# Gate rows first in a layer, and the output-gate products in halves between the steps of the matrix-memory core

## The chip, the cores and the metric

The kernel runs on one core of a Trainium2 chip. It is one program that goes twice through a loop over layers. The metric is the device time of one execution in microseconds (us); the time before is the median of three runs. Engines are called as in the profile: PE is TensorE (with PEld its weight loads), DVE is VectorE, ACT is ScalarE, POOL is GpSimd, SP is SyncE, which here only issues DMAs.

## What is computed

One inference step of a two-layer decoder. Each layer mixes 512 prompt tokens and 32 sampled tokens (8 sequences of 4), so N = 544 columns, by two mixers side by side, and then applies a feed-forward block. The part at issue is the matrix-memory mixer (mLSTM), with 4 heads of width 128:

```python
h = rmsnorm(x, W['norm1_g'][l])
u, v, o, ig, fg, q, kv, ng, ga, gb = split_cols(h @ W['w_in'][l])
...
c, conv_new = causal_conv(u, conv_buf, conv_w, conv_b)
q = jnp.einsum('bthd,hde->bthe', c, w_mq)
k = jnp.einsum('bthd,hde->bthe', c, w_mk) * (M_HEAD_DIM ** -0.5)
pre = jnp.concatenate([ig, fg], axis=-1).astype(jnp.float32) + b_gates.astype(jnp.float32)
i_pre = pre[..., :M_HEADS]
log_f = jax.nn.log_sigmoid(pre[..., M_HEADS:])
h, C, n, m = mlstm_chunkwise(q, k, v, i_pre, log_f, C0, n0, m0)
h = h * lax.rsqrt(jnp.mean(h * h, axis=-1, keepdims=True) + EPS) * norm_g...
out = h.reshape(B, T, M_WIDTH) * jax.nn.sigmoid(o.astype(jnp.float32))
```

`ig` and `fg` are the gate rows (8 rows in all): from them come, per token, the decays that the core needs. `o` is the output gate (512 rows): its sigmoid is needed only at the very end of the mixer, when the normalized core output is multiplied by it.

## The kernel before, in words

Every engine has its own instruction list, written out by hand; waits are on semaphores, and nothing but these lists and waits sets the order. Activations are kept feature-major: `hT` is the normed input as 8 chunks of 128 features by 544 columns. Weights arrive as units of 128 x 1024 floats (512 KB) in the order of the table `UNITS`, through a ring of 8 slots in SBUF that SP fills in order; before a slot is filled again SP waits in `unit_used` for its last user. A product writes a pair of PSUM banks (two halves of 272 columns); the table `GROUPS` numbers the products, and number modulo 4 is the pair. `begin` makes PE wait until that pair was read.

Some products are plain f32. The output gate, and many later ones, run in three passes of a split format: ACT casts a weight unit to a high part (`split_high`), DVE subtracts to get the low part (`split_low`), and likewise the input becomes `xh` (by ACT) and `xl` (by DVE; it takes the place of `hT`, so it must come after the last read of `hT`). `passes` then issues high times high, high times low and low times high, for each chunk and half: 48 matmuls of 272 columns per product.

A layer's first part is, on PE: the norm sum (L778); the four products `u` (L768, the first paced chunk by chunk by DVE, which writes `hT`); the value rows `tm` in token-major form (L826, L827); the gate rows `if` (L836); the four output-gate products `o` (L806); the query and key products `mq` and `mk` (L852), which ACT copies out (L1249); transposes of the gate rows (L863, wait for ACT's exponentials `wexp_ready`); the weighted keys `kw` (L872), which DVE copies out (L1543). Then comes the matrix-memory core: 4 heads of 5 steps, k = 0 to 19, with j = k modulo 5. In step k PE does the score product of step k+1 (L896), at j = 2 two spreads of gate rows over the partitions for the next head (L885, 4 rows of weights), then numerator and denominator of step k (L910, L911; at j = 4 eight 4-column products with the old state, L918), and at j = 4 the new state (L930, 32 rows). ACT makes the exponentials, DVE masks and multiplies them with the scores (`st_ready`) and, after a head's end, takes the reciprocal of its denominator (L1578). After the core PE sums the prompt state (L956), ACT copies it out (L1288), splits two query units (L1192), squares the heads' outputs (L1297), and PE takes their means (L968, `mn`); then the query products follow (L806).

ACT's chain for the gate rows (L1227 to L1233) and DVE's scans (L1511 to L1528) lie before the core and end in `rows_ready`.

## Time and profile before

| what | us |
|---|---|
| median of 3 runs | 2261.07 (2256.67, 2261.07, 2265.15) |
| the profiled execution: span from the first to the last instruction | 2255.4 |
| PE busy (share of the span) | 2113.5 (94%) |
| DVE, ACT, POOL busy | 934.4, 678.8, 103.4 |
| mean granted TensorE clock | 0.931 of 2.4 GHz |

The profile gives one execution; its span is what it has of that execution's own time, and the three timed runs lie 1.3 to 9.8 us above it. A busy PE is not PE at its peak: the ends of matmuls are modelled, and the granted clock is either 1.0 (2.4 GHz) or 0.5 (1.2 GHz), so that a stretch's mean says how much of it ran at which.

### The profile page before, as it was taken

The page shows a single profiled execution, that of the slowest core. Times are in us where ns is not written, and L with a number is a line of the kernel's source. Part 1 is how long each engine was busy: PE and PEld are TensorE (multiplying, and loading weights), DVE is VectorE, ACT ScalarE, POOL GpSimd, SP SyncE. Part 2 cuts the span into 40 slices and gives each one's busy share as a digit, 9 for nine tenths or more (in the row PEclk, how much of TensorE's full clock was granted, in tenths as well). Part 3 has the DMA queues.
Part 4 walks back from the last instruction along what each step waited for, and adds up shares of the span by engine and source line. Part 5 has one row for each costly group of instructions (what it writes and reads, how often), then busy time and mean ns, then how long its engine had stood idle before and what let it go on. Part 6 is the DMA issues. An engine that isn't in the chain of part 4 may idle for free. (4 is left out here: it accounts for less than half of the span.)

```text
span 2255.4 us, 34271 instructions
## 1 busy us (share of the span) xinstructions
PE 2113.5 (94%) x14028; PEld 1829.3 (81%) x14028; DVE 934.4 (41%) x1592; ACT 678.8 (30%) x1287; POOL 103.4 (5%) x144
## 2 busy tenths in 40 slices
PE   6989999999997999999779899999999979999996
PEld 5575884569997999999755758745799979999995
DVE  3144655643335332333222356556333453323333
ACT  2342235642223221222114323356422232212221
POOL 0012111000000000000000121110000000000000
PEclk9997897979998999999989979979799989999998
DMA  6211143002221222221042012510122212222211
GB/s 249 75 48 38 62 151 104 1 20 86 92 85 63 88 85 94 85 87 64 15 169 103 19 47 87 155 65 1 37 86 85 94 57 89 90 85 93 86 48 40
DMA packets 48114, 176.31 MB, mean 78 GB/s; under 512 B 6506, under 2 KB 6538, under 8 KB 47506
## 3 DMA queue, kind: packets, MB, share of 16 engines
q1 hardware_dynamic: 40754, 144.80, 19.0%
q0 software_dynamic: 7200, 29.27, 3.8%
q8 instruction: 114, 1.87, 0.3%
q14 instruction: 46, 0.38, 0.1%
HBM read 163.46 MB, written 14.71 MB: 79 GB/s over the span
## 5 line engine op out<-in xcount | busy, mean ns | idle before, releaser
L806 PE MATMUL ps<-xh,late_w 128*128 128x272 f32 x3840 | 650.0, 290 | 17.6 <-DVE xl L1803 15.7
L806 PEld LDWEIGHTS ps<-xh,late_w 128*128 128x128 f32 x3840 | 547.9, 190 | 21.3 <-issue 17.3
L1466 DVE TENSOR_TENSOR late_w<-ring,late_w 128x1024 fp32r<-128x1024 f32 x196 | 240.3, 1226 | 735.9 <-ACT late_w L1192 735.9
L1192 ACT CAST late_w<-ring 128x1024 fp32r<-128x1024 f32 x196 | 205.3, 1048 | 831.0 <-PE ps L806 830.9
L806 PE MATMUL ps<-xl,late_w 128*128 128x272 f32 x1920 | 398.8, 289 | 0.0
L806 PEld LDWEIGHTS ps<-xl,late_w 128*128 128x128 f32 x1920 | 304.8, 190 | 0.0
L806 PE MATMUL ps<-ah,late_w 128*128 128x272 f32 x1408 | 234.7, 288 | 0.0
L806 PEld LDWEIGHTS ps<-ah,late_w 128*128 128x128 f32 x1408 | 198.7, 188 | 0.0
L1331 ACT ACTIVATE slab<-ps,stat 128x31 f32<-128x31 f32 (+5 forms) x204 | 84.3, 449 | 117.2 <-DVE stat L1698 117.2
L806 PE MATMUL ps<-mh,late_w 128*128 128x272 f32 x576 | 98.9, 288 | 0.0
L996 PE MATMUL ps<-slab 64*128 64x512 f32 (+2 forms) x192 | 94.1, 618 | 0.0
L1033 PE MATMUL ps<-slab,vkv 128*64 128x256 f32 x320 | 91.3, 430 | 0.0
L1033 PEld LDWEIGHTS ps<-slab,vkv 128*64 128x64 f32 x320 | 44.2, 151 | 51.2 <-issue 34.9
L806 PEld LDWEIGHTS ps<-mh,late_w 128*128 128x128 f32 x576 | 82.4, 189 | 0.1
L768 PE MATMUL ps<-slab,ring 128*128 128x272 f32 x256 | 62.4, 407 | 21.2 <-DVE slab L1478 19.8
L826 PE MATMUL ps<-ring,slab 128*128 128x512 f32 (+1 forms) x160 | 81.7, 592 | 0.0
L806 PE MATMUL ps<-al_first,late_w 128*128 128x272 f32 x384 | 79.3, 288 | 0.0
L768 PEld LDWEIGHTS ps<-slab,ring 128*128 128x128 f32 x256 | 50.4, 198 | 33.9 <-issue 21.3
L1341 ACT ACTIVATE slab<-slab,stat 128x128 f32<-128x128 f32 (+4 forms) x140 | 69.0, 555 | 10.7 <-DVE stat L1721 10.4
L1015 PEld LDWEIGHTS ps<-const,slab 128*128 128x128 f32 (+1 forms) x384 | 42.9, 143 | 34.8 <-issue 23.4
L1015 PE MATMUL ps<-const,slab 128*128 128x128 f32 (+1 forms) x384 | 60.2, 297 | 6.6 <-ACT slab L1341 6.6
L806 PE MATMUL ps<-al_rest,late_w 128*128 128x272 f32 x320 | 66.2, 288 | 0.0
(298 smaller groups left out, 2911.8 us busy)
## 6 DMA issues: line engine op xcount, KB each, us to landing
ring<-in_W SPq DMA_DIRECT2D x262, 512.0 KB, 3.3
slab<-in_pages POOLq DMA_DIRECT2D x64, 128.0 KB, 2.5
slab<-in_c POOLq DMA_DIRECT2D x8, 512.0 KB, 9.5
out_sC<-slab POOLq DMA_DIRECT2D x8, 512.0 KB, 2.9
slab<-in_win POOLq DMA_DIRECT2D x2, 2048.0 KB, 8.6
out_oldwin<-in_cwin POOLq DMA_DIRECT2D x2, 2016.0 KB, 14.1
xT<-in_xT SPq DMA_DIRECT2D x8, 272.0 KB, 4.5
out_y<-slab SPq DMA_DIRECT2D x8, 272.0 KB, 2.1
```

The lines of the kernel that those rows point to most:

```text
L768: mm = pe.matmul(out[:, a, :], w[:, k, :], src[:, k, a * NHALF:(a + 1) * NHALF], start=(k == 0), stop=(k == kcs - 1))
L806: mm = pe.matmul(out[:, a, :], w[:, k * P:(k + 1) * P], x[:, a * NHALF:(a + 1) * NHALF], start=start, stop=stop)
L826: pe.matmul(ps[0:rows, s, :], x, w[:, 0:512], start=(k == 0), stop=(k == KC - 1))
L996: mm = pe.matmul(out[:, r], qrT[hd, r0 + r, i * P:(i + 1) * P], kT[hd, brs[0] - 1:brs[-1], 0:(i + 1) * P], start=True, stop=True)
L1015: mm = pe.transpose(ps[0:rows, 5 + x % 2, at:at + P], part, ident)
L1033: mm = pe.matmul(out, vkv[:, j, (br - 1) * P + g * HD:(br - 1) * P + (g + 1) * HD], PT[:, x % 2, 2 * c * P:2 * (c + 1) * P], start=(br == ...
L1192: act.copy(hi, ring[:, u % RING, :]).then_inc(wh_ready, 1)
L1331: ins = act.activation(prob(k)[:, r, :], score(k)[:, r, :], ACT.Exp, bias=stat[:, k % 3, r:r + 1], accum_out=stat[:, 3 + k % 3, r:r + 1] i ...
L1341: ins = act.activation(prob(k)[:, r, :], prob(k)[:, r, :], ACT.Copy, scale=stat[:, 8 + k % 3, r:r + 1])
L1466: dve.tensor_tensor(lo, ring[:, u % RING, :], hi.bitcast(F32), ALU.subtract).then_inc(wl_ready, 1)
```

## The change

In a layer, `if` comes first on PE, and is now the product that DVE's writes of `hT` pace; ACT's chain for the gate rows follows at once, before it reads out `u`. The four `o` products no longer stand between `if` and `mq`. Each is cut into two halves of 272 columns (`fill`: 24 matmuls into bank 5), and the eight halves stand on PE ahead of the numerator of the steps k = 0, 2, ..., 14. ACT copies each half out after its exponential of the next step, without the sigmoid, and takes one sigmoid over all four after the core. The split weights of `o` move into ring slots 1 to 4 (the last four `tm` units), so units after `o` get other slots, and SP holds the first `k` unit until all fills are done. The small product with `blk` moves behind the next head's first numerator (`new_n`), since bank 5 is now the fills'.

```diff
-UNITS = ([("u", m) for m in range(4)] + [("tm", k) for k in range(KC)] + [("if", 0)]
+UNITS = ([("if", 0)] + [("u", m) for m in range(4)] + [("tm", k) for k in range(KC)]
...
+FILL_BANK = 5
+FILLS = [(m, a) for m in range(4) for a in range(2)]
+def fill_at(k):
+    return k // 2 if k % 2 == 0 and k // 2 < len(FILLS) else None
...
+                        if UNITS[n] == ("k", K_ORDER[0]):
+                            sp.wait_ge(fill_done, len(FILLS))
...
+                    w = landed(("if", 0)).rearrange("p (k m) -> p k m", k=KC)
+                    out = begin(("if", 0))
+                    for k in range(KC):
+                        pe.wait_ge(h_ready, k + 1)
...
                     for m in range(4):
-                        fm("u", m, ready=(h_ready, 0))
+                        fm("u", m)
...
-                    for m in range(4):
-                        product3(("o", m), ("o", m), xh, xl, (xl_ready, 0)).then_inc(pair_done, 1)
+                    def fill(x):
+                        m, a = FILLS[x]
+                        n = SPLIT[("o", m)]
+                        pe.wait_ge(wl_ready, n + 1)
+                        if x >= 1:
+                            pe.wait_ge(fill_free, x)
+                        wh, wl, _ = split_weights(n)
+                        half = slice(a * NHALF, (a + 1) * NHALF)
+                        for k in range(KC):
+                            if x == 0:
+                                pe.wait_ge(xl_ready, k + 1)
+                            for w, y, start, stop in ((wh, xh, k == 0, False), (wh, xl, False, False), (wl, xh, False, k == KC - 1)):
+                                mm = pe.matmul(ps[:, FILL_BANK, 0:NHALF], w[:, k * P:(k + 1) * P], y[:, k, half], start=start, stop=stop)
+                        mm.then_inc(fill_done, 1)
...
+                        if fill_at(k) is not None:
+                            fill(fill_at(k))
                         numden(k)
+                        if j == 0 and h >= 1:
+                            new_n(h - 1)
...
-                    for m in range(4):
-                        if m < 2:
-                            split_high(m + 2)
-                        out, free = done(("o", m))
-                        act.activation(halves(haT[:, m, :]), out, ACT.Sigmoid).then_inc(free, 1)
...
+                        if k >= 1 and fill_at(k - 1) is not None:
+                            m, a = FILLS[fill_at(k - 1)]
+                            act.wait_ge(fill_done, fill_at(k - 1) + 1)
+                            act.copy(haT[:, m, a * NHALF:(a + 1) * NHALF], ps[:, FILL_BANK, 0:NHALF]).then_inc(fill_free, 1)
+                            if a == 1 and m < 2:
+                                split_high(m + 2)
...
+                    act.wait_ge(fill_free, len(FILLS))
+                    act.activation(haT[:, :, :], haT[:, :, :], ACT.Sigmoid).then_inc(sig_ready, 1)
...
-                    split_low(2)
-                    split_low(3)
+                    split_low(0)
+                    split_low(1)
+                    dve.wait_ge(pair_done, GROUP[("tm", TT)] + 1)
+                    for k in range(KC):
+                        dve.wait_ge(xh_ready, k + 1)
+                        dve.tensor_tensor(xl[:, k, :], hT[:, k, :], xh[:, k, :].bitcast(F32), ALU.subtract).then_inc(xl_ready, 1)
```

On PE, at the start of a layer, before (L768 is `u`, L826 and L827 are `tm`):

```order
L778 MATMUL ps<-acc,ones 128x272 x2
L768 MATMUL ps<-slab,ring 128x272 x64
L826 MATMUL ps<-ring,slab 128x512
L827 MATMUL ps<-ring,slab 128x280
L826 MATMUL ps<-ring,slab 128x512
```

and of the change (L862 is `if`, L810 is `u`, L876 and L877 are `tm`):

```order
L820 MATMUL ps<-acc,ones 128x272 x2
L862 MATMUL ps<-slab,ring 64x272 x16
L810 MATMUL ps<-slab,ring 128x272 x64
L876 MATMUL ps<-ring,slab 128x512
L877 MATMUL ps<-ring,slab 128x280
```

The 16 matmuls of `if` now stand ahead of the 64 of `u`. On PE, in the first head's steps 2 to 4, before (L910 and L911 are numerator and denominator, L899 and L896 scores, L918 the 4-column products):

```order
L910 MATMUL ps<-slab 128x256
L911 MATMUL ps<-slab,ones 128x256
L899 MATMUL ps<-slab 32x32
L910 MATMUL ps<-slab 128x128
L911 MATMUL ps<-slab,ones 128x128
L896 MATMUL ps<-slab 128x512
L914 MATMUL ps<-slab 128x32
L918 MATMUL ps<-slab 128x4 x8
```

and of the change (L898 are the fills, of which the last row of one and the first three of the next are shown):

```order
L898 MATMUL ps<-xh,gwl 128x272
L966 MATMUL ps<-slab 128x256
L967 MATMUL ps<-slab,ones 128x256
L955 MATMUL ps<-slab 32x32
L966 MATMUL ps<-slab 128x128
L967 MATMUL ps<-slab,ones 128x128
L952 MATMUL ps<-slab 128x512
L898 MATMUL ps<-xh,gwh 128x272
L898 MATMUL ps<-xl,gwh 128x272
L898 MATMUL ps<-xh,gwl 128x272
```

The order of the core's own rows is the same; 24 rows of a fill stand ahead of step 2 and of step 4. On ACT, after the core, before (L1267 and L1288 are copies out of PSUM, L1192 splits query units, L1297 squares):

```order
L1267 COPY slab<-ps 128x512
L1288 COPY slab<-ps 128x512
L1192 CAST qwh<-ring 128x1024 x2
L1297 ACTIVATE sq<-slab 128x544 x4
L1302 ACT_TABLE_LOAD
```

and of the change:

```order
L1331 COPY slab<-ps 128x512
L1358 COPY slab<-ps 128x512
L1360 ACT_TABLE_LOAD
L1360 ACTIVATE slab<-slab 128x2176
L1261 CAST qwh<-ring 128x1024 x2
L1369 ACTIVATE sq<-slab 128x544 x4
L1374 ACT_TABLE_LOAD
```

A table load and one sigmoid over 2176 columns now stand ahead of the splits and the squares.

## Rows read from the trace of the kernel before

**Rows 1.** The page's head: the span, and each engine's busy time.

```profile
span 2255.4 us, 34271 instructions
```

**Rows 2.** PE's waits, summed: waiting line, what it waited for, total, times, longest.

```profile
PE ps L885 <- ACT slab L1259: 6.0, 8, 0.8
```

**Rows 3.** PE by time, start of the first layer: start, length, row, idle before.

```profile
19.75 8.96 PE L768 MATMUL ps<-slab,ring 128*128 128x272 f32 x32 [5.37 <-DVE slab L1478]
30.14 22.27 PE L768 MATMUL ps<-slab,ring 128*128 128x272 f32 x96 [1.43 <-DMA ring<-in_W]
```

**Rows 4.** PE by time, from the gate rows to the core, first layer.

```profile
105.66 7.55 PE L836 MATMUL ps<-slab,ring 128*64 128x272 f32 x32
114.11 0.48 PE L806 MATMUL ps<-xh,gwh 128*128 128x272 f32 x2 [0.91 <-DVE xl L1506]
...
128.56 0.82 PE L806 MATMUL ps<-xh,gwh 128*128 128x272 f32 x2 [2.21 <-DVE gwl L1466]
...
130.08 0.66 PE L806 MATMUL ps<-xh,gwh 128*128 128x272 f32 x2
130.53 0.66 PE L806 MATMUL ps<-xl,gwh 128*128 128x272 f32 x2
...
142.11 3.83 PE L852 MATMUL ps<-slab,small 128*128 128x272 f32 x16
146.31 3.93 PE L852 MATMUL ps<-slab,small 128*128 128x272 f32 x16 [0.37 <-ACT slab L1249]
...
157.39 1.18 PE L885 MATMUL ps<-acc,const 4*128 4x272 f32 x4 [1.75 <-DVE slab L1543]
```

**Rows 5.** PE by time, the same place in the second layer.

```profile
1226.78 7.55 PE L836 MATMUL ps<-slab,ring 128*64 128x272 f32 x32
...
1261.74 3.83 PE L852 MATMUL ps<-slab,small 128*128 128x272 f32 x16
```

**Rows 6.** Windows: both cores of the program's two layers, and 4 us of the first.

```profile
157.40:246.20 88.80, 85.78 (x296) 54.61 (x296) 45.12 (x88) 18.85 (x48) 21.53 (x17) 0.73 0.10 36
177.00:179.00 2.00, 2.00 (x19) 1.98 (x18) 0.00 (x0) 0.00 (x0) 0.00 (x0) 1.00 0.00 0
181.00:183.00 2.00, 2.00 (x4) 0.67 (x3) 1.97 (x8) 0.20 (x1) 0.64 (x1) 0.50 0.00 0
1277.00:1366.00 89.00, 85.79 (x296) 54.64 (x296) 45.31 (x89) 19.03 (x49) 21.56 (x17) 0.73 0.10 36
```

The columns are: from and to, length, busy time of PE, PEld, DVE, ACT and POOL with their instructions, granted clock, share of the DMA engines, GB/s.

**Rows 7.** PE by time, in the core of the first layer and behind it.

```profile
176.93 1.95 PE L918 MATMUL ps<-slab 128*128 128x4 f32 x16
...
179.48 3.71 PE L930 MATMUL ps<-slab 32*128 32x512 f32 x4
...
249.41 6.51 PE L968 MATMUL ps<-sq,ones 128*128 128x272 f32 x16 [3.21 <-ACT sq L1297]
```

**Rows 8.** ACT by time, first layer.

```profile
106.58 1.99 ACT L1192 CAST gwh<-ring 128x1024 fp32r<-128x1024 f32 x2
...
122.75 0.62 ACT L1239 ACTIVATE slab<-ps 128x544 f32<-128x544 f32 x1
...
142.95 1.28 ACT L1242 ACT_TABLE_LOAD   x1
...
145.66 2.61 ACT L1249 ACTIVATE slab<-ps 128x544 f32<-128x544 f32 x5
...
246.72 1.99 ACT L1192 CAST qwh<-ring 128x1024 fp32r<-128x1024 f32 x2
248.61 1.20 ACT L1297 ACTIVATE sq<-slab 128x544 f32<-128x544 f32 x2
```

**Rows 9.** DVE by time, first layer.

```profile
113.24 5.17 DVE L1506 TENSOR_TENSOR xl<-slab,xh 128x544 fp32r<-128x544 f32 x8 [3.23 <-PE ps L836]
...
127.29 2.34 DVE L1466 TENSOR_TENSOR gwl<-ring,gwh 128x1024 fp32r<-128x1024 f32 x2
...
182.63 3.54 DVE L1578 RECIPROCAL slab<-slab 128x544 f32<-128x544 f32 x1
```

More of the change, by code:

```diff
@@ L80, with slot, turn, earlier @@
 UCOLS = 1024
+TURNS = UNIT[("q", 0)]
+def slot(n):
+    return n % RING if n < TURNS else (n - TURNS + UNIT[("o", 0)]) % RING
+def turn(n):
+    return sum(slot(x) == slot(n) for x in range(n))
+def earlier(n):
+    return max((x for x in range(n) if slot(x) == slot(n)), default=None)
 TMC = 512 + 280
-GROUPS = ([("n1", 0)] + [("u", m) for m in range(4)] + [("tm", i) for i in range(TT + 1)] + [("if", 0)]
-          + [("o", m) for m in range(4)] + [(w, h) for h in range(MH) for w in ("mq", "mk")]
+GROUPS = ([("n1", 0), ("if", 0)] + [("u", m) for m in range(4)] + [("tm", i) for i in range(TT + 1)]
+          + [(w, h) for h in range(MH) for w in ("mq", "mk")]
           + [("aw", 0)] + [("kw", i) for i in range(TT + 1)]
@@ L209, in al @@
             return al_first[:, k, :] if k < AL_FIRST else al_rest[:, k - AL_FIRST, :]
+        ring_at = where()
         ring = sb("ring", [P, RING, UCOLS])
+        gate_w = tuple(nc.alloc_sbuf_tensor_at(name, [P, 2, UCOLS], F32R, offset=ring_at + 4 * at * UCOLS)
+                       for name, at in (("gwh", 1), ("gwl", 3)))
         const = sb("const", [P, CONST_W])
@@ L321, in bc @@
             return ap.to_broadcast(shape)
+        assert [slot(UNIT[("tm", k)]) for k in range(4, KC)] == [1, 2, 3, 4] == [slot(UNIT[("k", m)]) for m in K_ORDER]
+        assert not {slot(UNIT[(w, m)]) for w in ("o", "q") for m in range(4)} & {1, 2, 3, 4}
         cos, sin, ident = con("cos"), con("sin"), con("ident")
@@ L371, in build_step @@
         h_ready = sem("h_ready")
+        fill_done = sem("fill_done")
+        fill_free = sem("fill_free")
+        sig_ready = sem("sig_ready")
+        n0_done = sem("n0_done")
         conv_ready = sem("conv_ready")
@@ L744, in landed @@
                         n = UNIT[key]
-                        pe.wait_ge(unit_landed[n % RING], 16 * (n // RING + 1))
-                        return ring[:, n % RING, :]
+                        pe.wait_ge(unit_landed[slot(n)], 16 * (turn(n) + 1))
+                        return ring[:, slot(n), :]
                     def begin(key):
@@ L812, in fm @@
                         product((kind, m), (kind, m), src, kcs, ready=ready).then_inc(pair_done, 1)
+                    w = landed(("if", 0)).rearrange("p (k m) -> p k m", k=KC)
+                    out = begin(("if", 0))
+                    for k in range(KC):
+                        pe.wait_ge(h_ready, k + 1)
+                        for a in range(2):
+                            mm = pe.matmul(out[0:64, a, :], w[:, k, 0:64], hT[:, k, a * NHALF:(a + 1) * NHALF],
+                                           start=(k == 0), stop=(k == KC - 1))
+                    mm.then_inc(pair_done, 1)
                     for m in range(4):
-                        fm("u", m, ready=(h_ready, 0))
+                        fm("u", m)
                     for i in range(TT + 1):
@@ L929, in new_state, with new_n @@
                         for a in range(2):
[L930 to L932 removed]
+                            mm = pe.matmul(ps[:, 6 + a, :], k, vb[0:NS, 4 * a:4 * a + 4, :], start=True, stop=True)
+                            if a == 1:
+                                mm.then_inc(cs_done, 1)
+                    def new_n(h):
+                        pe.wait_ge(den_read, h + 1)
+                        pe.matmul(ps[:, 4, 2 * NS:2 * NS + DECB], kw[0:NS, TT, h * MD:(h + 1) * MD], con("blk")[0:NS, :],
+                                  start=True, stop=True).then_inc(n0_done, 1)
                     nk = MH * (TT + 1)
@@ L1190, in split_high @@
                         u = UNIT[SPLITS[n]]
-                        act.wait_ge(unit_landed[u % RING], 16 * (u // RING + 1))
-                        act.copy(hi, ring[:, u % RING, :]).then_inc(wh_ready, 1)
+                        act.wait_ge(unit_landed[slot(u)], 16 * (turn(u) + 1))
+                        act.copy(hi, ring[:, slot(u), :]).then_inc(wh_ready, 1)
                     def root(key):
@@ L1198, in _ @@
                     root(("n1", 0))
+                    out, free = done(("if", 0))
+                    act.wait_ge(small_landed, 16)
+                    act.activation(halves(row(I_)), out[0:MH], ACT.Identity, bias=sml("bi")[0:MH, :])
+                    act.copy(halves(row(A_)), out[32:32 + MH]).then_inc(free, 1)
+                    read_out(act, ("if", 0))
+                    link(act.activation(row(Z_), row(A_), ACT.Identity, bias=sml("bf")[0:MH, :]))
+                    link(act.activation(row(L_), row(Z_), ACT.Abs))
+                    link(act.activation(row(A_), row(L_), ACT.Exp, scale=-1.0))
+                    act.activation(row(L_), row(A_), ACT.Ln, bias=ones[0:MH, 0:1]).then_inc(ln_ready, 1)
                     for m in range(4):
@@ L1605, in _ @@
                             masked(k + 2)
+                        if k in (3, 7):
+                            split_low(2 if k == 3 else 3)
                         if j == 0 and h >= 1:
```

49 lines of the change are left out of this document (15 added, 34 removed).

## The prediction, made blind

> **What bounds the kernel now.** I read the page first, then PE's waits, then PE by time around the gate rows and through the core, then windows of the granted clock, and last ACT and DVE at the same places. The span is 2255.4 us [rows 1]; the median of the runs, 2261.07, is 5.7 us more, so I make the sum as a difference on the profiled execution and add it to the median. PE is busy nearly all of the time, and what the change touches is one stretch per layer: from the gate rows' product to the end of the core. In the first layer that product starts at 105.66 and takes 7.55, the four output-gate products run from 114.11 to 142.11, `mq`, `mk`, the transposes and `kw` fill the time to 157.39, where the core's first spread starts [rows 4]; the core ends at about 246.2, and the means follow at 249.41 after a wait of 3.21 for ACT's squares [rows 7]. The reader should see two things. First, PE has hardly any wait in the core that another product could fill: the largest kind is the spread's wait for ACT, 8 times 0.7 to 0.8, 6.0 us in both layers together [rows 2]. Second, PE runs much of the core at the lower clock: both cores have a mean granted clock of 0.73 over 88.8 and 89.0 us [rows 6]. With levels of 1.0 and 0.5 that is 2 x 0.27 x 88.8 = 48 us at half clock per layer, which costs 24 us.
>
> The clock falls after certain work, not after waiting. At 177 to 179, in the 4-column products with the old state (from 176.93), it is still 1.00; in the new state's 32-row products (from 179.48) it has fallen, and at 181 to 183 it is 0.50 with PE busy 2.00 of 2.00 us [rows 6, 7]. The Trainium skill, page "TensorE: Matmul & The Clock Gate", section "Why this matters for your kernels", advises to avoid long idle gaps between bursts of matmuls, because they bring the clock down. By that rule a PE with no idle row would keep the full clock here and the core would have nothing to win; the trace disagrees, with 0.50 at full busy time, and the measurement decides.
>
> **The change, part by part.**
>
> *Gate rows first.* DVE paces the first product: `u` number 0 takes 19.75 to 28.71 (30.14 less the wait of 1.43) = 8.96, while an unpaced `u` takes 22.27 / 3 = 7.42 [rows 3]. Now `if` (7.55 unpaced [rows 4]) stands in the paced place, and all four `u` come after it. The front becomes 7.4 us longer, and the 7.55 at 105.66 go: nothing in sum. The chain that ACT and DVE make of the gate rows goes from the end of `if` (113.21) to well before ACT's first output-gate sigmoid at 122.75 [rows 4, 8], under 10 us for ACT; it now lies beside `u`, which has 7.4 us per product, and DVE's scans beside `tm`. It costs nothing in either place; were its cover gone, PE would wait for it at the transposes. The ring takes the units in the new order one product later and needs them one product later, so SP's queue of loads stays as far ahead.
>
> *The output-gate stage goes.* From 113.21 to 142.11 it is 28.9 us in the first layer, 1261.74 - (1226.78 + 7.55) = 27.4 in the second [rows 4, 5]; mean 28.2. This includes the waits of 0.91 and 2.21, and a piece at half clock. The 15.28 us from `mq` to the first spread remain, with one new wait. ACT starts two splits about 0.9 us after PE's last value row (106.58 against 105.66) and takes 1.99; then come its table load and exponentials, 142.95 to 145.66 = 2.71; the first copy-out of `mq` takes 0.62. Those 0.9 + 2.0 + 2.7 + 0.6 = 6.2 us now start when PE starts `mq`. PE can do four products, 3.83, until it needs a pair back: it waits 2.4, of which 0.37 were there before [rows 4, 8]. So 2.0 us are given back, and I take 0.5 for a clock that falls in the new wait (0 to 1.5). DVE has two splits (2.34) and `xl` (5.17) at that time [rows 9], 7.5 us, which end before `kw` needs it. Net per layer: -28.2 + 2.5 = **-25.7**.
>
> *The fills.* The same 192 matmuls return in the core. Two whole products took 114.11 to 126.35 (128.56 less 2.21), 12.24 for 96 matmuls, 0.1275 each; at half clock a pair starts 0.45 after the last (130.08 to 130.53), 0.225 each [rows 4]. Eight fills of 24 cost 24.5 us at full clock, 43.2 if all at half. They hide in nothing: the spreads' waits stand ahead of them and remain. So they add 24.5 unless the clock changes. The edges between the two forms of matmul I take as nothing; a first pair takes 0.48 against a spacing of 0.26 [rows 4], so 16 edges of 0.2 would be at most 3 us.
>
> *The clock in the core.* Both places after which it falls, the spreads and the old and new state, stay in each head, in their order. So I keep two slow stretches per head at about their length: fills then run partly in them, and the rest of the core's work runs outside them instead. Fills are dense and may end a slow stretch somewhat sooner; I take a tenth of the 48 us, which gives back 2.4. Bounds: 24 back if the half clock went altogether, 18.7 more if every fill were slow and the rest as before. I take a value near nothing since the rows that cause the falls are unchanged: **+24.5 - 2.4 = +22.1**.
>
> *ACT and DVE inside the core.* Eight copies of at most 0.6, two splits of 1.0 on ACT [rows 8] and 1.2 on DVE [rows 9]. What is behind them is the next exponential, and behind that DVE's product for the step after. A copy follows its fill while PE does that step's numerator, the next scores and the next step's numerator, whose exponential is already made; then comes the next fill, 3.1 us. So nothing waits. In the third head the fill at j = 0 even covers DVE's reciprocal of 3.54 [rows 9]. Uncovered, these would cost 8 x 0.6 + 2 x 2.2 = 9 us per layer.
>
> *The sigmoid behind the core.* Before, ACT goes from its copy-out straight to two splits (246.72, 1.99) and the squares (248.61) for which PE waits [rows 7, 8]. Now a table load of 1.28 and a sigmoid over 2176 columns come first. 544 columns take 0.62, 1024 about 1.0 [rows 8], so about 0.8 ns per column: 0.62 + 1632 x 0.8 ns = 1.9. PE waits 3.2 us longer, in full: **+3.2** (2.5 to 4).
>
> *The rest.* `new_n` is a moved 8-column product. SP holds the `k` units until the last fill, some 20 us ahead of the core's end, and they are used only after four query products; what queues behind them is used later still. Nothing.
>
> *Sum.* Per layer -25.7 + 22.1 + 3.2 = -0.4; two layers -0.8; 2255.4 - 0.8 = 2254.6, or 2261.07 - 0.8 = **2260.3** against the median.
>
> **The rivals.**
>
> *The fills keep the clock up (faster).* Dense products between the slow pieces leave fewer falls. For it: the output-gate stage itself, dense, runs mostly at 0.1275, and the core's dense pieces bring the clock back each time. Against it: at 157.39 and later the falls come after pieces that stay. If half of the 48 us goes, 12 per layer instead of 2.4: 2 x 9.6 = 19 faster than my sum, 2241. It beats the bound of 0.5% (11 us, about what a measurement of this kernel can tell from no change) once more than about 15 of the 48 us go (2.0 - 15.3 / 2 = -5.6 per layer). The same page of the Trainium skill, section "Loop structure matters more than you think", says that a following group of matmuls right behind keeps the array warm; this is the case it would give.
>
> *The fills run slow (slower).* The fills at k = 2 and 12 stand directly behind spreads, after which the clock falls. If slow stretches grow with them so that half of all fill time is at half clock on top of the old 48 us: 9.4 us per layer, plus the 2.4 not won: 2 x 11.8 = 24 slower, 2284. It decides from about 6 us more per layer. For it: after the old state the clock stays down through the new state's rows as well. Against it: a fill is the densest work that the kernel has.
>
> *The fills hide more than I see (not what I expect, faster).* If the modelled ends of PE's rows cover waits for DVE's or ACT's results inside the core, fills fill them. With as much per layer unseen as both layers show (6.0 [rows 2]) it is 12 faster, 2248. Against: the core's steps at full clock start at the spacing of their columns.
>
> **How the numbers follow.** Near zero as summed: 0.56, its own range 2249 to 2272 (the two layers' clock terms may each be off by 5). Faster by clock or by hidden waits: 0.25. Slower by slow fills, or by ACT's copies and splits coming late (18 us in both layers): 0.19. The range that holds 8 in 10 takes in the half-won clock and a half of the slow case: 2241 to 2278. Faster by over 0.5% 0.25, within 0.56, slower 0.19.
>
> **What would show it.** The first spread starts about 18 us after the last value row. The core lasts about 111 us, with a mean clock near 0.80 (1 - 0.5 x 43 / 111). Fill rows at 0.125 to 0.13 spacing in more than half of their time. The wait for the squares is about 6.4 us. I am wrong if the core's clock rises over 0.85 or falls under 0.73, or if fills start after waits for `fill_free` or the scores' products.

## The result, and the profile after

The changed kernel takes 2262.86 us (median of 20 runs) against 2260.39 of the kernel before (20 runs). The medians differ by 2.5; the ratio worked out from all of these runs is 1.0018, with a 95% interval from 1.0011 to 1.0024: 2.5 to 5.4 us slower, 4.1 in the middle. The forecast was 0.8 faster, so the size (almost nothing) was right and the sign was not. The profiled execution has a span of 2260.2 us, 4.8 more than in [rows 1].

PE's waits by line, summed (total, times, longest); before, only the first of these kinds was there in this size [rows 2], and the squares cost 3.21 a layer [rows 7]:

```profile
PE ps L941 <- ACT slab L1323: 6.0, 8, 0.8
...
PE ps L1037 <- ACT sq L1369: 13.1, 2, 6.5
...
PE ps L908 <- ACT slab L1313: 4.7, 2, 2.4
...
PE ps L966 <- DVE slab L1672: 2.8, 5, 1.2
```

L941 are the spreads, L1037 the means, L908 the query and key products, L966 the numerators. The spreads' waits are what they were. The other three are longer or new. Of the numerators' five waits one is at the second head's first step; the other four are in the last head's second and third steps, two in each layer, behind the last fill (PE, then DVE, first layer):

```profile
168.66 2.04 PE L966 MATMUL ps<-slab 128*128 128x512 f32 x2 [1.21 <-DVE slab L1672]
...
228.52 0.91 PE L966 MATMUL ps<-slab 128*128 128x384 f32 x2 [0.72 <-DVE slab L1672]
```

```profile
223.71 3.54 DVE L1649 RECIPROCAL slab<-slab 128x544 f32<-128x544 f32 x1
...
227.92 0.55 DVE L1672 TENSOR_TENSOR slab<-ps,slab 128x384 f32<-128x384 f32 x1
```

DVE's product for the last head's second step stands behind its reciprocal for the head before, and no fill covers it there.

PE by time, from the start of the first layer to the core (answers to [rows 3, 4]):

```profile
20.09 10.30 PE L862 MATMUL ps<-slab,ring 128*64 128x272 f32 x32 [5.38 <-DVE slab L1550]
...
113.11 0.64 PE L877 MATMUL ps<-ring,slab 128*32 128x280 f32 x2
113.67 3.93 PE L908 MATMUL ps<-slab,small 128*128 128x272 f32 x16
119.96 5.62 PE L908 MATMUL ps<-slab,small 128*128 128x272 f32 x16 [2.35 <-ACT slab L1313]
...
132.72 1.18 PE L941 MATMUL ps<-acc,const 4*128 4x272 f32 x4 [1.74 <-DVE slab L1613]
```

The gate rows now stand in the paced place, and the query products follow the last value row at once. Their second half waits 2.35 and then takes 5.62, where the same 16 matmuls took 3.93 before. From the first query product to the first spread it is 132.72 - 113.67 = 19.05, before 157.39 - 142.11 = 15.28 [rows 4]. In the second layer (1233.92 to 1252.97) it is 19.05 again.

Windows of the two cores, of the query products behind their wait, and of the means (columns as in [rows 6]; the granted clock is the third number from the end):

```profile
132.70:243.60 110.90, 105.80 (x488) 77.84 (x488) 51.97 (x90) 23.35 (x58) 21.44 (x17) 0.83 0.15 53
1253.00:1365.90 112.90, 109.18 (x488) 79.22 (x488) 50.13 (x90) 23.36 (x58) 21.51 (x17) 0.80 0.16 56
...
121.50:124.50 3.00, 3.00 (x8) 2.21 (x7) 1.61 (x3) 1.05 (x2) 0.00 (x0) 0.50 0.10 40
250.50:254.50 4.00, 4.00 (x10) 2.92 (x10) 0.40 (x1) 1.06 (x3) 0.00 (x0) 0.51 0.81 250
1373.00:1377.00 4.00, 4.00 (x10) 3.03 (x9) 0.18 (x1) 1.22 (x2) 0.00 (x0) 0.50 0.86 251
```

The cores are 22 and 24 longer than in [rows 6], at 0.83 and 0.80 instead of 0.73. In this execution both pieces that follow a lengthened wait run at the lower level.

ACT and then PE behind the core (answers to [rows 7, 8]; the last row is the second layer's):

```profile
243.66 0.59 ACT L1358 COPY slab<-ps 128x512 f32<-128x512 f32 x1 [7.74 <-PE ps L1026]
244.26 1.28 ACT L1360 ACT_TABLE_LOAD   x1
245.56 2.02 ACT L1360 ACTIVATE slab<-slab 128x2176 f32<-128x2176 f32 x1
247.48 1.97 ACT L1261 CAST qwh<-ring 128x1024 fp32r<-128x1024 f32 x2
249.36 1.20 ACT L1369 ACTIVATE sq<-slab 128x544 f32<-128x544 f32 x2
```

```profile
243.34 0.28 PE L1026 MATMUL ps<-ones,rstd 128*128 128x1 f32 x2
250.16 6.01 PE L1037 MATMUL ps<-sq,ones 128*128 128x272 f32 x16 [6.53 <-ACT sq L1369]
256.98 0.50 PE L848 MATMUL ps<-xh,qwh 128*128 128x272 f32 x2 [0.81 <-ACT rstd L1374]
...
1372.43 6.36 PE L1037 MATMUL ps<-sq,ones 128*128 128x272 f32 x16 [6.53 <-ACT sq L1369]
```

Table load and sigmoid take 3.3, and PE's wait grows by just that. Put together, each stage as a difference to before, in the profiled executions (starts on PE; a layer begins with its norm sum at 12.57 and 1125.79, before at 12.22 and 1125.78):

| stage | forecast, per layer | first layer | second layer |
|---|---|---|---|
| norm sum to first spread | -25.7 | -25.0 | -24.1 |
| core | +22.1 | +22.1 | +24.1 |
| end of core to first query product | +3.2 | +3.3 | +5.2 |
| from there to the layer's end | 0 | -0.7 | -0.5 |

### The profile page after: what moved, and what is told of

It reads as the page before. It is cut to its first block and busy times, and to the rows that moved or that the text cites. A ratio compares the mean times of both kernels' runs of the same rounds, so it can differ in the third digit from the quotient of the medians.

```text
span 2260.2 us, 34309 instructions
## 1 busy us (share of the span) xinstructions
PE 2110.8 (93%) x14028; PEld 1829.4 (81%) x14028; DVE 940.8 (42%) x1592; ACT 683.4 (30%) x1297; POOL 103.2 (5%) x144
## 5 line engine op out<-in xcount | busy, mean ns | idle before, releaser
L876 PE MATMUL ps<-ring,slab 128*128 128x512 f32 (+1 forms) x160 | 81.7, 592 | 0.0
L848 PE MATMUL ps<-ml,late_w 128*128 128x272 f32 x320 | 65.9, 287 | 0.0
L1769 DVE TENSOR_TENSOR ps<-ps,const 128x256 f32<-128x256 f32 (+4 forms) x76 | 32.5, 428 | 71.1 <-PE ps L1065 39.6
```

The costliest lines, as they stand in the source:

```text
L848: mm = pe.matmul(out[:, a, :], w[:, k * P:(k + 1) * P], x[:, a * NHALF:(a + 1) * NHALF], start=start, stop=stop)
L876: pe.matmul(ps[0:rows, s, :], x, w[:, 0:512], start=(k == 0), stop=(k == KC - 1))
L1769: return dve.tensor_tensor(t, t, bc(mask.unsqueeze(1), [P, parts_of(k), width_of(k) - lo]), ALU.add)
```

## Experiments

Differences in us to the changed kernel are worked out from the ratios to the kernel before, times 2260. The changed kernel's own ratio is 1.0018, and 1.0015 in a second measurement (last of the experiments); the second is used for the kernels that were timed beside it (late splits the second time, "steps only", and "fill between, no fill at a head's start"). With the intervals of both ratios each difference is good to 3 to 5 us either way (an estimate, the intervals added in squares). "Core" is from the first spread to the end of the prompt state's sums, first and second layer.

**The sigmoid behind the core.** First left out, then made another way:

```diff
-act.activation(haT[:, :, :], haT[:, :, :], ACT.Sigmoid).then_inc(sig_ready, 1)
```

> The changed kernel, but the sigmoid over 2176 columns behind the core (and with it its table load) is left out: the output gate's products go into the last multiplication as they are. Theory (the tail costs what the waits show): core and front stay as they are, PE's wait for the squares falls from 6.5 back to 3.2 in each layer, and the kernel gets 2 x 3.3 = 6.6 us faster than the changed one, up to 9 if the means of the second layer come back to the full clock as they had it before; it is then 3 to 6 us faster than the kernel before. Rival (the loss is in the core or ahead of it, and what the tail gives back is eaten by a PE that starts its means at a lower clock): less than 3 us faster than the changed kernel.

Ratio 0.9988 (0.9977 to 0.9998): 6.8 faster than the changed kernel. The wait for the squares is 3.21 again in both layers. The tail costs what the waits show.

```diff
-act.copy(haT[:, m, half], ps[:, FILL_BANK, 0:NHALF])
+act.activation(haT[:, m, half], ps[:, FILL_BANK, 0:NHALF], ACT.Exp, scale=-1.0)
...
-link(dve.reciprocal(rstd, rstd))
-link(qm = qm * mng * rstd)
-haT = haT * qm
+link(haT = (haT + 1.0) * rstd)
+link(dve.reciprocal(haT, haT))
+haT = qm * mng * haT
```

> The changed kernel with the gate made another way: ACT copies each half out as exp(-x), with the table that the core's exponentials have loaded, and behind the core DVE makes (1 + e) times the root, its reciprocal and one multiplication, three operations per head as before; no sigmoid and no table load stand ahead of the squares. Theory: an exponential on the copy-out costs what the copy costs (0.39), so the core stays as it is and the time is that of the kernel without the sigmoid, within 1.5 us: 6 to 9 us faster than the changed kernel. Rival (the exponentials from PSUM or the three operations on DVE are longer or late): the gain over the changed kernel is under 3 us and PE waits for DVE behind the means.

Ratio 0.9989 (0.9977 to 1.0000), 6.6 faster. The exponential out of PSUM takes 0.40 where the copy took 0.39. ACT and PE behind the core of this kernel:

```profile
245.34 0.58 ACT L1358 COPY slab<-ps 128x512 f32<-128x512 f32 x1 [10.41 <-PE ps L1026]
245.83 1.99 ACT L1261 CAST qwh<-ring 128x1024 fp32r<-128x1024 f32 x2
247.72 1.20 ACT L1366 ACTIVATE sq<-slab 128x544 f32<-128x544 f32 x2
```

```profile
248.52 4.07 PE L1037 MATMUL ps<-sq,ones 128*128 128x272 f32 x16 [3.21 <-ACT sq L1366]
```

Here, in the first layer, the means run at the full clock, in 4.07; in the second they take 5.59. From the core's end to the first query product it is 13.35 to 13.37 in all 22 layers of the eleven profiles with the wait of 6.5, and 8.1 to 10.0 (mean 8.9) in the twelve layers of the six with the wait of 3.2, the kernel before among them. So the longer wait costs 4.4 on the mean by the profiles: 3.3 of waiting, and the rest because the means behind it start at the half clock in all 22 layers, behind the shorter one in 3 of 12. The times of the two kernels (6.8 and 6.6 for both layers, 3.3 to 3.4 a layer) are too coarse to tell this from the wait alone.

**The price of the fills.** The loop over the 8 chunks of a fill keeps only the first:

```diff
-for k in range(KC):
-    for w, y, start, stop in (...):
+for w, y, start, stop in ((wh, xh, True, False), (wh, xl, False, False), (wl, xh, False, True)):
```

> The changed kernel with only 3 of the 24 matmuls in each half product (the first chunk of 128 features; the other seven are left out), so that 168 of 192 per layer are gone and all copies, splits and waits stay. Theory (fills cost their full-clock spacing and the core's slow time stays about what it was): 168 x 0.1275 = 21.4 us per layer go, 43 in both, and the core falls from 111 to about 90 us at a mean clock near 0.73, as before the change. Rival A (fills cost what their starts show, 32 us per layer, because part of them runs at half clock and nothing else got quicker): 28 per layer, 56 in both. Rival B (the fills hide waits that the modelled ends of PE's rows conceal): under 17 per layer, and new waits of PE show in the core.

Ratio 0.9925 (0.9904 to 0.9945), 21 faster, below all three. Windows of its two cores:

```profile
131.80:225.90 94.10, 91.09 (x320) 58.70 (x320) 47.55 (x90) 23.31 (x58) 21.59 (x17) 0.73 0.18 66
1243.90:1338.80 94.90, 88.24 (x320) 57.22 (x320) 50.62 (x90) 23.32 (x58) 21.46 (x17) 0.75 0.19 67
```

The cores are 34.8 shorter together. At 0.73 and 0.75 they hold 98 us at the half clock, the changed kernel's 83: without the fills the clock is as low as before the change. Take these 15 / 2 = 7.7 out, and 336 matmuls cost 42.5, 0.126 each: about the forecast price. The rest of the surprise lies behind the cores: from the first query product to the layer's end this kernel takes 8.2 and 7.4 longer than the changed one. Windows from 80 to 160 us behind that product, first of the changed kernel, then of this one:

```profile
336.98:416.98 80.00, 74.49 (x285) 40.40 (x286) 45.57 (x122) 45.70 (x150) 11.20 (x21) 0.83 0.24 76
```

```profile
319.25:399.25 80.00, 74.92 (x279) 41.38 (x275) 39.61 (x109) 41.60 (x138) 12.99 (x22) 0.74 0.28 87
```

Nearly the same rows (285 and 279 matmuls) with the same busy time run at 0.74 instead of 0.83. That is seen; why the clock of a later stage differs was not found.

**The gate rows first, alone.** The product and its chain move as in the change; the output-gate products stay whole and ahead of `mq`.

> The kernel before with one part of the change alone: the gate rows' product comes first in a layer and ACT's and DVE's chain for it follows at once; the four output-gate products stay whole and in their place ahead of the query and key products, with their sigmoid. Theory (the two places cost the same): no change from the kernel before, within 2 us. Rival (the gate rows in the paced place, or their chain beside u and the value rows, cost something that the sum took as nothing): 2 us slower or more, and the start of the output-gate products lies later than before by 1 us or more in each layer.

Ratio 1.0020 (1.0008 to 1.0033), 4.5 slower than before. The start of a layer is not it: from the norm sum to the end of value rows and gate rows it takes 113.09 - 12.60 = 100.49, before 113.21 - 12.22 = 100.99 [rows 4]. But the first output-gate product starts late:

```profile
118.15 0.79 PE L806 MATMUL ps<-xh,gwh 128*128 128x272 f32 x2 [5.06 <-DVE xl L1530]
```

In the old place the gate rows' 7.55 covered ACT's and DVE's splits: DVE began `xl` as soon as the gate rows ended (113.24 [rows 9]), and PE waited 0.91 for it [rows 4]. Moved alone, that cover is gone: DVE's splits now run behind the last value row, `xl` begins 4 us later than that row's end, and PE waits 5.06. In the change the first fill needs `xl` only at 139.40, 26 us behind the last value row.

**The new wait ahead of the core.** The two splits go behind the copies that PE waits for (and DVE's behind `kw`):

```diff
-split_high(0); split_high(1)
 act.wait_ge(rows_ready, 1)
...
 act.activation(halves(dst[:, h, :]), out, ACT.Copy, scale=scale).then_inc(free, 1)
+split_high(0); split_high(1)
```

> The changed kernel with one place of ACT's and DVE's lists altered: the two splits of output-gate units, which stand between the last value row and the exponentials that the query and key products' copies follow, move behind those copies (on DVE behind the weighted keys). The first fill needs them only some 14 us later. Theory (the wait of 2.35 that the change brought ahead of the second half of these products also lowers PE's clock there: from the first of these products to the first spread it is 19.05 us, and 15.28 before the change, so 3.8 instead of the 2.5 that the prediction took): the wait falls to about 0.4 and the stretch to 15.3 to 15.7, so the kernel gets 2 x 3.5 = 7 us faster than the changed one. Rival A (the stretch is longer for another reason, so that only the wait itself goes): 2 x 2 = 4 us faster. Rival B (the splits are now late for the first spreads or the first fill): waits of PE appear there and the gain is under 2 us.

> The kernel with the two splits behind the copies once more. Its profiled execution took 2251.2 us, the fastest of its twelve, while their median was 2259.9, so its profile does not show where the gain of its shorter stretch ahead of the core (19.05 to 15.48 in both layers) went in most executions. Theory (the stretch is shorter in every execution, and what is lost again is clock behind it, which differs from execution to execution): the stretch is 15.5 again, the median is 2257 to 2261, and a profiled execution near the median shows more time at the lower clock in the core or the attention part than the first profile. Rival (the first timing was low in its gain by chance): the median is about 7 us below the changed kernel's.

The stretch ahead of the core is 15.48 in all four profiled layers. PE there:

```profile
112.64 3.94 PE L908 MATMUL ps<-slab,small 128*128 128x272 f32 x16
117.04 3.93 PE L908 MATMUL ps<-slab,small 128*128 128x272 f32 x16 [0.46 <-ACT slab L1311]
```

So the wait can lower the clock, but it does not each time. Eleven profiles have the wait of 2.35 in both layers. Behind it the second half takes 5.5 or 5.6 in 14 of their 22 layers (all of the second layers, 3 of the first) and 3.93 or 3.94 in the other 8. Behind waits of 0.37 to 0.46 it is 3.93 or 3.94 in all 14 layers of seven profiles. The changed kernel's second profile, first layer, has the same wait and no slow piece:

```profile
119.71 3.93 PE L908 MATMUL ps<-slab,small 128*128 128x272 f32 x16 [2.35 <-ACT slab L1313]
```

The stretch ahead of the core is then 17.4 instead of 19.05; over the eleven profiles it is 18.4 on the mean, 3.1 over the 15.28 before. The two ratios with late splits are 1.0004 (0.9994 to 1.0013) and 0.9993 (0.9983 to 1.0003): 3 and 5 faster than the changed kernel. The 7 of the theory took the slow piece for certain; by the mean stretch, 2 x 2.9 = 6 was to be won, which the measurements do not exclude. The second profile, near its median, has cores of 113 and 113 at 0.82 and 0.80, like the changed kernel's second profile, and 4.3 more behind the first of them than the changed kernel's first. That part of the gain is lost to the clock further on, as the theory there has it, is possible, and not shown: the first profile of this kernel has no such loss.

**The fills in PE's waits.** Four fills stand between the two spreads of a head, three ahead of a head's first numerator:

```diff
+FILL_AT = (0, 2, 4, 5, 7, 10, 12, 15)
...
 spread(h + 1, 0)
+fill(fill_at(k))
 spread(h + 1, 1)
```

> The changed kernel with the eight half products at other steps of the core: four stand between the two spreads of a head (where PE waits 0.70 to 0.78 for ACT's copy, 8 times), three ahead of the first numerator of a head (where it waits up to 1.2 for DVE's product), one stays at the fifth step; on ACT the second part of the spread's copy moves behind the step's exponentials. The work is the same. Theory (the core has only these waits, and a half product of 3.1 us covers them wholly): the 6.0 and most of the 2.8 us of waits go, and nothing else changes: 6 to 9 us faster than the changed kernel. Rival A (PE stays as long at its lower clock or longer, since the spreads are now apart and each of them ends in a stretch at half clock): no gain, core as long as before at a mean clock under 0.80. Rival B (the second spread's copy is late for the head's end): new waits of PE in the core of as much as went.

Ratio 0.9949 (0.9937 to 0.9961): 15.6 faster, far more than the waits. Windows of its cores:

```profile
130.00:235.90 105.90, 104.87 (x488) 78.59 (x488) 49.23 (x90) 23.16 (x58) 21.56 (x17) 0.84 0.17 60
1246.90:1349.10 102.20, 101.72 (x488) 76.15 (x488) 50.24 (x90) 23.16 (x58) 21.51 (x17) 0.87 0.17 62
```

The waits in the core fall from 8.8 to 1.5, and the clock rises to 0.84 and 0.87. Five more runs ask which part did that:

> The changed kernel with the half products at the steps of the kernel with fills in the waits (0, 2, 4, 5, 7, 10, 12, 15), but behind both spreads of a head, so that the spreads stand next to each other as in the changed kernel, with their waits of 0.70 to 0.78. It tells apart what gave that kernel 16 us where its waits explain 6 to 9. Theory (spreads that follow each other directly bring the clock down; a half product between them keeps it up): this kernel wins only the waits ahead of the heads' first numerators, 2 to 3 us against the changed kernel, and its core runs at about 0.80 to 0.83. Rival (a half product at a head's first step, behind the old and the new state, is what brings the clock back): it wins 8 us or more, and the core's clock is 0.84 or over.

> Four half products between the two spreads of a head as in the kernel with fills in the waits, and the other four at steps 4, 9, 14 and 16, none at a head's first step. Theory of the spreads: the 6.0 us of waits go and the clock stays up behind the spreads, 12 to 16 us faster than the changed kernel, core clock 0.84 to 0.87. Rival of the heads' first steps: only the waits go, 4 to 6 us faster, and the core's clock is 0.83 or less.

> The changed kernel, but the second spread of a head goes into banks of its own, so that it follows the first at once without the wait of 0.70 to 0.78 for ACT's copy; the numerator of that step comes ahead of the half product, which now waits for the copy of the bank that the second spread uses. The spreads stand next to each other as before, only the idle time between them is gone. Theory of the waits (idle time in the core brings the clock down): the core falls to about 106 us at a clock of 0.84 to 0.86, 12 us or more faster than the changed kernel. Rival of the work (the spreads' matmuls with 4 rows of weights, next to each other, bring it down whether PE waits or not): only the waits go, core 108 to 111 at 0.80 to 0.83, 3 to 6 us faster.

> The changed kernel with the numerator and denominator of the step (about 1.1 us at the full clock) set between the two spreads of a head, and the first scores between those of the first head; the half products stay at the changed kernel's steps, behind the second spread. It takes the spreads apart and covers the waits, without half products between them. Theory of the waits: as without waits above, core about 106 us at 0.84 to 0.86, 12 us or more faster than the changed kernel. Theory of neighbourhood (spreads that stand apart do not bring the clock down): the same, 12 us, while the kernel with neighbouring spreads without waits wins only 3 to 6. Rival (it takes a dense piece as long as a half product between them): 4 to 6 us faster, core at 0.83 or less.

> The kernel with the numerator between the two spreads once more, since its first profile took 2246.9 us, the fastest of twelve executions whose median was 2258.7. Theory (a short product covers the waits and no more; a half product is needed to keep the clock up): the median is 2256 to 2260 again, and in an execution near it the core is 108 to 110 us at 0.80 to 0.83. Rival (taking the spreads apart keeps the clock up by itself): the core is about 106 or less at 0.84 or over, and the first profile is the rule.

| kernel | spreads of a head | waits in the core, both layers | core, us | clock | ratio (95%) | to the changed kernel |
|---|---|---|---|---|---|---|
| changed | neighbours, wait | 8.8 | 110.9, 112.9 | 0.83, 0.80 | 1.0018 | |
| steps only | neighbours, wait | 6.0 | 111.6, 110.1 | 0.80, 0.81 | 0.9995 (0.9985 to 1.0005) | -4.5 |
| no wait | neighbours | 1.2 | 108.3, 106.0 | 0.81, 0.82 | 0.9979 (0.9967 to 0.9990) | -8.8 |
| numerator between (first time) | apart by 1.1 us | 0 | 106.4, 103.4 | 0.82, 0.85 | 0.9999 (0.9986 to 1.0011) | -4.3 |
| numerator between (second time) | apart by 1.1 us | 2.6 | 108.6, 109.3 | 0.81, 0.81 | 0.9994 (0.9980 to 1.0009) | -5.4 |
| fill between, no fill at a head's start | apart by 3 us | 4.3 | 105.9, 105.9 | 0.85, 0.85 | 0.9967 (0.9954 to 0.9980) | -10.8 |
| fill between | apart by 3 us | 1.5 | 105.9, 102.2 | 0.84, 0.87 | 0.9949 (0.9937 to 0.9961) | -15.6 |

The first profile of the kernel with the numerator between lay 11.8 under that kernel's median, so its cores are those of an unusually short execution. Windows of the kernel with neighbours and no wait, then of the one with the numerator between, first and second time:

```profile
129.90:238.10 108.20, 106.99 (x496) 78.98 (x496) 48.79 (x90) 23.56 (x62) 21.51 (x17) 0.81 0.17 59
1248.80:1354.80 106.00, 106.00 (x496) 77.77 (x496) 47.49 (x90) 23.68 (x62) 21.51 (x17) 0.82 0.17 60
```

```profile
129.80:236.20 106.40, 106.33 (x488) 76.72 (x488) 47.58 (x91) 23.36 (x59) 21.62 (x17) 0.82 0.16 60
1249.70:1353.10 103.40, 103.35 (x488) 74.37 (x488) 47.58 (x91) 23.37 (x59) 21.53 (x17) 0.85 0.16 56
```

```profile
130.50:239.10 108.60, 107.36 (x488) 77.40 (x488) 49.01 (x90) 23.34 (x58) 21.45 (x17) 0.81 0.16 59
1252.90:1362.20 109.30, 107.87 (x488) 77.46 (x488) 49.01 (x90) 23.34 (x58) 21.51 (x17) 0.81 0.16 58
```

These kernels have between none and 2.6 us of waits left (the 2.6 are numerators again), and in five of the six cores the clock is 0.81 or 0.82, within the changed kernel's 0.80 to 0.83. In the second core with neighbours and in both of the first numerator profile PE has no wait at all, and the clock is 0.82, 0.82 and 0.85: the core stays at half clock for a good part without any idle time. So the theory that the waits bring the clock down falls.

A half product between the spreads brings it up. Counting all profiles, the clock is 0.80 to 0.83 (mean 0.81) in the 16 cores of the eight with whole fills and neighbours that wait, 0.81 to 0.85 (mean 0.82) in the six cores without that wait, and 0.82 to 0.87 (mean 0.85) in the eight cores of the four with a half product between (two of them further down). The times agree at both ends: 11 and 16 faster with a half product between, about 5 with the numerator between or with the steps alone. Two things stay open. The ranges touch, and one short execution had 0.85 with only the numerator between; and 9 faster with neighbours and no wait is not told apart from the 11. With a half product between, ACT's second copy also moved behind the exponentials; that was not run by itself.

**Together.**

> Two of them: gate as exp(-x), and the two splits behind the copies; the half products stay at the changed kernel's steps. Theory: 7.6 (measured for the gate alone) + 7 = 14 to 15 us faster than the changed kernel, 11 to 12 faster than the one before. Rival (the two do not add): under 10 faster than the changed kernel.

> The three alterations together: gate as exp(-x) without a sigmoid behind the core, splits behind the copies of the query and key products, half products in the core's waits. Theory (they act in different stretches and add): 7 + 7 + 6 = 20 us faster than the changed kernel, some 17 faster than the one before. Rival (the clock behind the core is what ends up paying: PE at the half clock more often in the attention part when it was dense longer): half of it, 8 to 12 us.

The two: 0.9948 (0.9930 to 0.9966), 15.8 faster than the changed kernel. All three: 2233.92 us, 0.9884 (0.9868 to 0.9899), 30 faster than the changed kernel and 26 faster than before. The three alone gave 7, 3 to 5 and 16, so they add within the errors; the rival (half of it) falls.

> The kernel with all three alterations (gate as exp(-x), late splits, half products in the waits), and ACT takes the first two squares ahead of the two splits of query units behind the core. Theory (the wait for the squares decides at which clock the means run: 6.0 to 6.9 us long at half clock behind every wait of 6.5, 4.07 to 6.7 behind waits of 3.2): the wait falls from 3.2 to about 1.2 and the means run in 4.1 to 5 us, 2 to 4 us per layer, 4 to 8 in both, faster than the kernel with all three. Rival (the query units split later are then what PE waits for): a wait for the low part ahead of the first query product, and under 2 us gained.

2233.19 us (4 runs), 0.9876 (0.9860 to 0.9892), 2 faster than the kernel with all three, with an error of about 5: no gain that can be told, and 6 not excluded. Locally the theory held: the first wait for the squares is 1.3, the means run at the full clock (each pair of them 2.07 long), and from the core's end to the first query product it is 6.9 instead of 10.0 in both layers. The rival did not show. In the profile, which is the slowest of the four runs, the first core takes 4 longer (at 0.82 instead of 0.87) and the first layer behind its first query product 6.5 longer than in the kernel with all three; why is open.

**The change once more.**

> The changed kernel itself once more, on the chip of the three others. Theory (three small terms are what the sum missed: clock behind the new wait ahead of the core, means at half clock, and a core that is no shorter than summed): again 1 to 4 us slower than the kernel before; the stretch from the first query product to the first spread is about 19 us in both layers again, the core 110 to 113, the wait for the squares 6.5. Rival (the loss was one execution's clock): ratio within 0.999 to 1.001 and other lengths in the stretch ahead of the core.

Ratio 1.0015 (1.0004 to 1.0026). Core 113.4 and 112.6, wait for the squares 6.5, but the stretch ahead of the core is 17.4 in the first layer and 19.05 in the second: the 19 of the theory came once in two, for the wait of 2.35 does not lower the clock each time. The loss itself came again, and the rival (one execution's clock) falls.

## Why the prediction was right or wrong

The parts of the change were right and their sum was not, because it is a difference of -0.4 a layer between terms of 25, and three terms were too kind by about 1 us each. The steps that failed are the half microsecond for the clock in the new wait, "So nothing waits" in the core, and a price for the sigmoid without the slow piece behind it.

*Gate rows first: 0 in sum.* Right for the layer's start (101.18 against 100.99). The prediction did not see that these rows covered the splits in their old place; the gate rows moved alone show that cover at 4.5 us, and the change happens not to need it.

*The output-gate stage, -25.7.* The new wait was found and sized (2.4 forecast, 2.35 measured). The step that failed is "I take 0.5 for a clock that falls in the new wait (0 to 1.5)". Where the clock falls, 16 matmuls take 5.62 instead of 3.93: 1.7, outside the bounds, and 3.8 us are given back instead of 2.5. Where it does not, it is 0. In 14 of 22 layers it falls, so the term is 1.2 on the mean, 0.7 more than taken; the changed kernel's profile has it in both layers. The runs with late splits show that the wait is the cause: without it, no layer has the slow piece.

*The fills, +24.5.* Right: 0.126 each against 0.1275. With that the rival that they hide unseen waits falls too.

*The clock in the core, -2.4.* About right: 0.83 and 0.80 against 0.80 forecast. The half clock went from 48 us a layer to 38 and 45, which gives back 3.3 (3.9 by the run with thin fills), 0.9 more than taken. "The clock falls after certain work, not after waiting" held in the core, where cores without a wait still run at 0.82 and 0.85; it did not hold ahead of the core and behind it, where the clock is low behind waits. What the prediction lacked is that the place of the fills decides. "They hide in nothing" is true of the steps chosen, and 16 us off for others.

*ACT and DVE in the core: "So nothing waits."* This step failed. The numerators wait 2.8 us in both layers for DVE's product, 1.4 a layer that the sum has at nothing; before, the core had no such wait. The prediction saw that a fill covers DVE's reciprocal in the third head, and not that the second and the last head have no fill at their first step: there the waits are. With the half products at other steps ("steps only") this wait is gone, the clock is no higher, and the kernel is 4.5 faster, with an error of 3.

*The sigmoid behind the core, +3.2 (2.5 to 4).* The wait was right (6.4 forecast, 6.53 measured). The means behind it were taken at the clock they had; behind the longer wait they always start at half clock, so the term is 3.3 and 5.2 in the profile, and 4.4 by all profiles, 1.2 more than taken. Part of this is luck of the profile before: its means ran slow in the first layer and at full clock in the second. Without the sigmoid the change would be 2 to 3 us faster than the kernel before: this term decides the sign.

Put together from the mean terms, -0.4 + 0.7 - 0.9 + 1.4 + 1.2 = +2.0 a layer, 4 us slower in both; measured were 4.1. That the agreement is so close is in part luck: each term is good to about half a microsecond.

Two of the three are one mistake: a wait of PE was costed by its length alone, or nearly, and not with the slow stretch behind it. The Trainium skill, page "TensorE: Matmul & The Clock Gate", section "Why this matters for your kernels", warns of idle gaps that bring the clock down. The prediction set that against the core, where the traces do disagree with it; behind the wait of 6.53 they agree, with 0.50 at the start of the means in all 22 layers, and behind the wait of 2.35 in 14 of 22. The Trainium skill, same page, section "Loop structure matters more than you think", has it that matmuls right behind keep the array warm. The half product between the spreads bears this out (0.85 on the mean); the short numerator there hardly does (0.81 to 0.85, mean 0.82).

Of the rivals, "the fills keep the clock up" is what the same fills do at other steps: with four of them between the spreads the half clock falls from 48 us a layer to about 30, more than the 15 that the rival asked for, and the kernel is 11.5 faster than the one before. "The fills run slow" did not come.

## What to carry to other kernels

Cost a wait of the matrix engine with what may run behind it at the lower clock, not by its length alone: here 2.0 us more of wait ahead of the core cost 2.1 in some layers and 3.8 in others, and 3.3 more behind it cost 4.4 on the mean. Work that is to fill an engine's gaps has to stand in the gaps: the same eight half products at other steps, four of them between the spreads and three at heads' starts, were worth 16 us. Before an activation that needs another table is put on the path, look whether the loaded table can make it (here an exponential, with three operations as before on the next engine).

## What the runs showed of the hardware

A stage's granted clock differs between executions and kernels at nearly the same work: the attention part had 0.83 in one profile and 0.74 in another with the same busy time. From the first query product to the layer's end, where these kernels run the same products on PE, the eighteen profiles take 868 to 877 us in the first layer and 879 to 888 in the second, and one profiled execution may lie 9 to 12 us from its kernel's median. So a gain of 6 us, seen row by row in one profile, is near what the times here can tell from nothing, and has to be measured again.

The core runs at the lower clock for a good part even where PE has no idle row in it (0.82, 0.82 and 0.85), and behind a wait of 6.53 the means start at half clock in all 22 layers, behind one of 3.21 in 3 of 12. An exponential from PSUM over 272 columns takes what a copy takes (0.40 and 0.39).
